# Two groups of adaLN modulation units moved in a hybrid diffusion trunk step: one outside the weight ring, one to VectorE

## The reference

```
sh1, sc1, g1, sh2, sc2, g2 = split(silu(cond) @ ada_w[l] + ada_b[l], 6)
h = rms_norm(x, norm1_g[l]) * (1 + sc1) + sh1
out = even_mixer(h) if l == 0 else odd_mixer(h)
x = x + g1 * out
h = rms_norm(x, norm2_g[l]) * (1 + sc2) + sh2
x = x + g2 * ((silu(h @ w1) * (h @ w3)) @ w2)
```

## Time and profile before

| | |
|---|---|
| median of 3 runs | 1096.36 us (1094.56, 1096.36, 1099.53) |
| profiled execution | 1100.81 us, span 1098.9 us |
| TensorE busy | 1053.1 us, 96% |
| weight loads of TensorE (PEld) | 982.2 us, 89% |
| VectorE busy | 664.2 us, 60% |
| GpSimd busy | 562.2 us, 51% |
| ScalarE busy | 421.3 us, 38% |
| chain that ended last | PE 81%, DVE 8%, POOL 3%, DMA 3%, ACT 3% |

### The profile page before, as it was taken

How to read it: one execution, slowest core, us unless ns; L and a number is a source line. 1 busy time by engine, 2 the same in 40 slices (tenths; PEclk the granted TensorE clock), 3 DMA queues, 4 the chain that set the end, 5 groups by cost and what they waited for, 6 DMA issues and landing times.

```text
span 1098.9 us, 16466 instructions
## 1 busy us (share of the span) xinstructions
PE 1053.1 (96%) x6510; PEld 982.2 (89%) x6510; DVE 664.2 (60%) x1346; ACT 421.3 (38%) x713; POOL 562.2 (51%) x422
## 2 busy tenths in 40 slices
PE   4999989997999999999999999898999999999997
PEld 2898889885999999999999998665999999999997
DVE  3698897328767887878787544387655653231222
ACT  4352232457424433333223344486344333333221
POOL 0454568461345555555666444103635656665562
PEclk9899999999999999999999999999999999999999
DMA  9454434356838766675566731502246544434341
GB/s 333 155 184 150 139 133 154 119 177 212 260 102 243 206 198 190 197 228 161 152 201 196 180 79 32 136 2 78 77 133 192 166 123 115 116 91 151 113 126 58
DMA packets 220488, 166.41 MB, mean 151 GB/s; under 512 B 20269, under 2 KB 208764, under 8 KB 220284
## 3 DMA queue, kind: packets, MB, share of 16 engines
q1 hardware_dynamic: 188480, 132.59, 40.7%
q10 hardware_dynamic: 31932, 32.77, 9.3%
HBM read 162.43 MB, written 2.92 MB: 150 GB/s over the span
## 4 chain that ended last, share of the span: by engine, by line
PE 81%; DVE 8%; POOL 3%; DMA 3%; ACT 3%; issue 1%; ACTq 0%; SPq 0%; DVEq 0%
PE banks L508 21%; PE banks L510 20%; PE banks L509 20%; POOL w_lo L1280 3%; PE banks L579 2%; PE banks L581 2%; PE banks L580 2%; PE banks L819 2%; PE banks L625 2%; DMA raw<-in_ada_w 1%; DVE xg_lo L1870 1%; ACT w_hi L1304 1%; PE banks L602 1%; PE banks L1122 1%; DMA raw<-in_w_in_even 1%; PE banks L1138 1%
## 5 line engine op out<-in xcount | busy, mean ns | idle before, releaser
L1280 POOL TENSOR_TENSOR w_lo<-raw,w_hi 128x512 fp32r<-128x512 f32 (+2 forms) x393 | 530.5, 1379 | 514.8 <-ACT w_hi L1304 514.8
L508 PE MATMUL banks<-xg_hi,w_hi 128*128 128x386 f32 (+1 forms) x784 | 271.5, 346 | 6.8 <-DVE xg_lo L2033 6.5
L510 PE MATMUL banks<-xg_hi,w_lo 128*128 128x386 f32 (+1 forms) x784 | 266.8, 340 | 0.0
L509 PE MATMUL banks<-xg_lo,w_hi 128*128 128x386 f32 (+1 forms) x784 | 266.3, 340 | 0.0
L1304 ACT ACTIVATE w_hi<-raw 128x2048 fp32r<-128x2048 f32 (+5 forms) x110 | 185.3, 1685 | 193.8 <-PE banks L510 135.8
L508 PEld LDWEIGHTS banks<-xg_hi,w_hi 128*128 128x128 f32 x784 | 149.1, 190 | 11.0 <-issue 7.1
L509 PEld LDWEIGHTS banks<-xg_lo,w_hi 128*128 128x128 f32 x784 | 148.8, 190 | 0.5
L510 PEld LDWEIGHTS banks<-xg_hi,w_lo 128*128 128x128 f32 x784 | 149.1, 190 | 0.0
L508 PE MATMUL banks<-h_hi,w_hi 128*128 128x384 f32 (+1 forms) x376 | 130.3, 346 | 3.5 <-POOL w_lo L1280 3.4
L509 PE MATMUL banks<-h_lo,w_hi 128*128 128x384 f32 (+1 forms) x376 | 126.5, 336 | 0.0
L510 PE MATMUL banks<-h_hi,w_lo 128*128 128x384 f32 (+1 forms) x376 | 126.4, 336 | 0.0
(11 more groups left out here) (381 smaller groups left out, 1618.2 us busy)
## 6 DMA issues: line engine op xcount, KB each, us to landing
raw<-in_ffn_w SPq DMA_DIRECT2D x88, 512.0 KB, 5.2
vada_raw<-in_ada_w ACTq DMA_DIRECT2D x24, 1024.0 KB, 5.8
raw<-in_ffn_w SPq DMA_DIRECT2D x32, 704.0 KB, 4.6
raw<-in_ada_w SPq DMA_DIRECT2D x20, 1024.0 KB, 6.8
raw<-in_w_in_even SPq DMA_DIRECT2D x18, 1024.0 KB, 5.2
shift<-in_ada_w SPq DMA_DIRECT2D x4, 1024.0 KB, 12.1
raw<-in_w_out_even SPq DMA_DIRECT2D x4, 1024.0 KB, 6.7
raw<-in_w_in_odd SPq DMA_DIRECT2D x3, 1024.0 KB, 5.3
```

Source lines behind the costliest of these rows:

```text
L508: pe.matmul(out, s_hi, m_hi, start=first and j == 0, stop=False)
L509: pe.matmul(out, s_hi, m_lo, start=False, stop=False)
L510: mm = pe.matmul(out, s_lo, m_hi, start=False, stop=last and j == len(terms) - 1)
L1280: ins = pool.tensor_tensor(low_part(s)[:, at:to], raw[u % RAW][:, at:to], high(s)[:, at:to].bitcast(F32), ALU.subtract)
```

## The change

The first mixer's gate (group 2) no longer goes through the ring. Once the bank of group 0 is filled, ScalarE starts the four transfers into the buffers of the shift; TensorE does the products after input features 6 and 7 (two units each); VectorE waits for them before it sets `SF`. Group 5 goes to VectorE: the first FFN has 24 units in place of 20 there, with 6 or 7 steps an up unit in place of 5 or 6, from the second unit on in place of the third, and 11, 10, 9, 8, 7, 6, 4 steps at the first seven down tiles in place of 7 (and 8 at the seventh). The second FFN's steps, 4 a unit, start one unit earlier too.

```diff
-ADA_PLACES = {"start": 8, "levels": 4, "mlstm": 8, "mlstm_norm": 2, "norm1": 2, "ffn0": 20, "ffn1": 4}
+ADA_PLACES = {"start": 8, "levels": 4, "mlstm": 8, "ffn0": 24, "ffn1": 4}
...
-SUMS_FROM = 2
-SUMS_UP = [5 + f % 2 for f in range(SUMS_FROM, 22)]
-SUMS_DOWN = [(8 * VADA - sum(SUMS_UP) + m) // 7 for m in range(7)]
+SUMS_FROM = 1
+SUMS_UP = [6 + f % 2 for f in range(SUMS_FROM, 22)]
+SUMS_DOWN = [11 - m for m in range(6)]
+SUMS_DOWN += [8 * VADA - sum(SUMS_UP + SUMS_DOWN)]
...
     for i in range(4):
-        ada("levels", i, i + 1)
         if i == 0:
...
     ada("mlstm", 4)
-    ada("mlstm_norm")
     add("out0", 1, DT, 256, 2)
...
     add("up0", 1, DT, 256, 1)
-    ada("norm1")
     add("up0", FT - 2, DT, 256, 2)
...
+            def level_gate(i):
+
+                pe.wait_ge(S[f"levels_in{i}"], 16)
+                mm = strips(ada_bank(8 + i), i, shift_raw[i].rearrange("p (k n) -> p k n", k=2))
+                if i == 3:
+                    mm.then_inc(adas.done, 1)
...
             for j in range(6, 12):
                 features(("in0", j), *in0(j * P))
+                if j < 8:
+                    level_gate(2 * j - 12)
+                    level_gate(2 * j - 11)
...
             for j in range(6, 18):
-                if 9 <= j < 13:
-                    modulation("levels", j - 9, j - 8)
...
-            modulation("mlstm_norm")
             first_outputs(0, 8, 6, DT)
...
             out_projection(0)
-            modulation("norm1")
             ffn(0, 16)
...
             split_to(3)
+            adas.filled(act, ("ada", 0))
+            for n in range(4):
+                act.dma_start(shift_raw[n].rearrange("p (k n) -> p k n", k=2),
+                              I["ada_w"][0].rearrange("(k p) n -> p k n", p=P)[:, 2 * n:2 * n + 2, 2 * D:3 * D]).then_inc(S[f"levels_in{n}"], 16)
             first_norm()
...
                 .then_inc(S["n0_in"], 1)
+            adas.filled(dve, ("ada", 2))
             dve.memset(SF[:], 1.0)
             step(dve.memset(PX[:], 1.0))
...
-            modulation("mlstm_norm")
             biases_to(5)
...
-            modulation("norm1")
             dve.wait_ge(S["s_out"], 16)
```

More of the change, by code:

```diff
@@ L426, in build @@
                "neg_max", "p_ready", "pv_hi", "masks_ready")
+        signal("levels_in0", "levels_in1", "levels_in2", "levels_in3")
         signal("shift_in0", "shift_in1", "shift_in2", "shift_in3", "ss_ready", "diag_ready", "gain0", "xg0_hi", "xg0_ready",
```

## The result

The change makes the kernel slower by a little: 1099.81 us against 1096.27 us (medians of 19 runs each), ratio 1.0025 with a 95% interval of 1.0014 to 1.0036, or +3.5 us. The prediction was 1093.1 us, 3.3 us faster: the wrong direction, though inside its range. The profiled execution of the changed kernel took 1100.68 us (span 1099.1), almost what the profiled one of before took.

A forecast was written before the change was run, and what follows sets the result against it. TensorE was taken to bound the kernel nearly everywhere. Terms -4.6 + 0.4 + 0.6 + 1.3 - 0.5 - 0.5 = -3.3 us, applied to the 1096.36 median, gave 1093.1 us; 8-in-10 range 1087.5 to 1101.

The forecast's parts named there:

- the -4.6 of part 1: Level stage: gate units out of the ring remove the late transfer and the 13.05 us matmul block's excess, -4.6 us.
- The third rival: Level stage: stall only partly the transfer's, TensorE still waits for POOL in one block; +1.3, 1097.7 us, chance 0.12.
- the 0 of part 4 for the second unit's seven steps: First FFN, second unit: seven steps where there were none cost 0, its bank not being wanted for two more tiles.
- VectorE's load a unit: First FFN: VectorE needs 8.2 us a unit against TensorE's 9.25, so the added steps cost 0.
- Part 4's arithmetic: First FFN's gate to VectorE: two pairs of products less, -3.74, four column sums more, +3.24, together -0.5 us.
- The down tiles' 0: First FFN's down tiles: up to eleven steps lag under 2 us, covered by three banks, costing 0.
- both waits in the mixer: VectorE makes TensorE wait before the first level product, +0.6 us, and at the fifth level, +1.3 us.
- the late weights: Mixer: four gate transfers share bandwidth with the next mixer weights near 54 to 57 us, +0.4 us, bounds 0 and 2.
- the last tile: First FFN's last down tile: four steps instead of eight remove TensorE's idle time before the column sum, -0.5 us.
- The chain: VectorE's forget-gate chain in the mixer, begun later, meets fewer POOL pieces and lasts 26.8 us instead of 32.2.
- the second wait: Fifth level: less slack and earlier POOL pieces beside VectorE cost +1.3 us, half of 2.5, bounds 0 and 4.
- VectorE late twice in the mixer: Rival: 3.5 us at the first level, slow clock 1.6, 3.0 at two levels; +2.9, 1099.3 us, chance 0.18.

The follow-up runs named there:

- run 12: The kernel before the change, nothing edited, one more profiled execution: 1096.21 us (span 1094.3).
- run 1: The kernel before with only the mixer's gate units taken out of the ring: 1096.84 us against 1096.25, ratio 1.0001.
- run 4: The changed kernel, nothing edited, one more profiled execution: 1099.98 us (span 1098.3).
- run 11: Changed kernel, all four mixer gate units before input feature 6, FFN steps from third up unit, down tiles 10, 10, 10, 9, 9, 8, 6: 1096.49 us, before 1096.52.
- run 5: Kernel before with only the FFN part, steps from the third up unit, down tiles 12, 11, 10, 9, 8, 7, 5: 1099.58 us against 1097.01.
- run 6: The kernel before with only the down tiles' steps changed to 8, 8, 8, 7, 7, 7, 5: 1096.49 us against 1097.01, ratio 0.9988.
- run 7: The kernel before with only the mixer part, all four gate units ahead of input feature 6: 1095.33 us against 1097.01, ratio 0.9979.
- run 2: The kernel before with only the FFN part of the change: 1098.21 us against 1096.25, ratio 1.0023.
- run 3: The kernel before the change, nothing edited, one more profiled execution: 1098.41 us (span 1096.5).

## Why the prediction was wrong, point by point

**The step that failed most is the -4.6 of part 1.** The block of the earlier trace rows was read as what this kernel does, and it is what two of six executions do. The late transfer did go, as part 1 has it (no split waits for one in the level stage of any of the eight profiles), but TensorE had mostly not been waiting for it: in run 12 the block lasts 8.45 us although ScalarE waited 8.98 us. The removal is worth nothing that the medians show (run 1). The prediction had the hint: it said that the profiled execution lay 4.4 us above the median of the runs, and the excess of the block was 4.6. It applied the forecast difference to the median all the same, and so took the stall off a number that did not hold it. The third rival had the doubt but tied it to POOL being held up in every execution; in fact it is held up in some, when its last piece begins just before a row of operations on VectorE. Without this term the prediction's own sum is -3.3 + 4.6 = +1.3.

**The second is the 0 of part 4 for the second unit's seven steps.** It looked at the bank and not at ScalarE's queue. Measured: 1.26 to 1.29 us as one wait and, with the chase behind it, 3.3 us (run 4 against run 11). Before has a chase of 1.8 us there that went with group 5 out of the ring, so the net is +1.5; the prediction had neither. The point that I did look at, VectorE's load a unit, held: with six or seven steps a unit from the third on (run 11), TensorE has no idle time in the up units.

**Part 4's arithmetic left out what TensorE waits for at the places that were emptied.** The -3.74 and the +3.24 are right (-2.76 ahead of the FFN with a wait of 0.85 in it; 24 column sums in place of 20). The wait of 0.83 to 0.86 us ahead of the first up unit is in every run with group 5 gone from that place and in none with it there: its products had covered the time in which VectorE works at the residuals. The first down tile was not seen either: 0.33 us of idle time, 0.65 us longer from column sum to column sum (13.02 against 12.37).

**The down tiles' 0 held, barely.** Eleven steps first left no wait; twelve (run 5), or four tiles of 10, 10, 10 and 9 (run 11), gave 1.0 us at a column sum.

**Right:** the kind and place of both waits in the mixer and the size of the first (0.66 for 0.6), the late weights (+0.2 for +0.4, within bounds), and the last tile (-0.5, run 6). VectorE's memsets began at 78.13 (forecast near 77). TensorE came to the first level at 102.78 (forecast 102.3) and got its operands 0.66 later. The chain took 26.1 us (78.13 to 104.26, forecast 26.8). One reading under it was wrong: the memsets did not take their 1.34 us without POOL, which was at its pieces from 62.52 to 67.56 beside the first of them; they are simply not slowed by it, in after either. The size of the second wait (1.40 for 1.3) is partly luck: 1.3 was half of a bound, the pieces came 4 us earlier and not 8, and two products on VectorE cost 1.03 more each. The mixer's sum without the stall, +2.3, was +1.5 in run 4; relief of the chase by the moved products, as in run 7, would explain that, but no run isolates it.

**A hit for the wrong reason:** the rival *VectorE late twice in the mixer* gives 1099.3 us, close to the measured 1099.81, but its waits of 3.5 and 3.0 us and its slow clock are not there. Most of the loss is in the FFN part (2.0 us in run 2), where that rival has none.

**The sum again, with what the runs showed:** mixer +1.5; ahead of the FFN -2.76; in the FFN four column sums +3.24, the second unit's steps +3.3, the chase of before that went -1.8, the first down tile +0.65, the last -0.55, and the transposes that went -0.25; together +3.3, measured +3.5 at the last column sum. The remaining 0.2 us is not assigned.

## What to carry to other kernels

When the profiled execution lies above the median by the size of a stall that the argument rests on, take a second profile or leave the stall out of the sum. When work is added to one engine, follow the next instruction of every engine that waits for its result, in that engine's own order: the price here was paid by a split that has nothing to do with the added sums. Small waits of TensorE behind a producer that it has caught up with are worth looking for in the weight loads; unrelated products put in front of such a block cost less than their own time (1.3 us less in run 7), while the same products behind features 6 and 7 also start another engine's chain too late.

## What the runs showed of the hardware that I had not expected

The same four pieces of the same work took 10.58 and 10.50 us in two executions and 4.97 to 5.71 in four others. A piece on POOL that began 0.4 to 0.5 us before a row of VectorE's operations was held for 6.8 to 6.9 us, past several of them (0.94 us each, none slowed), and one that began 0.30 us after the first of them took 2.00 us and made VectorE's second take 2.04. How long POOL needs where it meets VectorE is not fixed by the program: in these six executions it goes with under a microsecond of difference in when the last piece begins.

TensorE's clock after a wait does not go by the length of the wait alone. After 3.02 us and 1.93 us it read 0.50, the 1.2 GHz level. After 1.78 us (before, wait ending at 263.22) it stayed at 1.00, and so it did after 1.40 us (kernel after, fifth level) and 1.02 us in run 11; after 1.00 us in run 5 it read 0.59 and 0.56 in the two stretches from 551 to 555. That single fall cost 1.6 us, more than the wait before it. And the same two waits of 0.63 us near 674 in the kernel before were followed by 0.57 in run 3 and by 1.00 in run 12.
